# Scores of the 128-key units in three matmuls instead of five, low halves beside the mask, one rotary step a filler later

## Chip, cores and metric

The kernel runs on one core of a Trainium2 chip. The metric is the device time of the whole program in microseconds; before the change the median of 3 runs is 680.2 us (680.0 to 680.59).

## What is computed

The reference is one encoder block over 512 tokens of width 2048, in float32:

```
h = rms_norm(x);  a_q, a_k, a_v, a_g, b_cq, b_ckv, b_kr, b_g = split(h @ w_in)
A: sliding window attention, 16 heads of 64, window 128 in chunks of 64, one sink logit per head
B: qb = rms_norm(b_cq) @ w_q_b -> 8 heads x (128 "nope" + 64 rotary)
   kvb = rms_norm(b_ckv) @ w_kv_b -> 8 heads x (128 key + 128 value); one rotary key (64) for all heads
   s = (q_nope . k_nope + q_rope . k_rope) / sqrt(192)
   s = -1e30 where key chunk > query chunk (chunks of 64);  p = softmax(s);  o = p @ v
out = rms_norm(x + concat(A * silu(a_g), B * silu(b_g)) @ w_out)
```

## The kernel before

Float32 accuracy is kept with halves: each operand is split in a high part (rounded to the matmul's format fp32r) and a low part (the rest), and a product is three matmuls, high x high, low x high, high x low (`three`, L1076). ScalarE makes the high halves, VectorE or GpSimd the low ones. Weights come as a stream of 128x1024 chunks: a DMA into `w_raw`, ScalarE's `w_hi` (L364), GpSimd's `w_lo` (L283).

The order of work on each engine is written out by hand; every engine waits on semaphores only. The input projections and branch A come first (to about 402 us), then branch B, then the output projection (up to the end), each fed by the same stream.

Branch B has 8 heads in 4 pairs (pair 0 to 3), and a pair has 8 score units. Unit w = 8p + u has query block i = u % 4 of head u // 4, and 128 (i + 1) keys, because later keys are masked. So units with u = 0 and u = 4 have 128 keys, 8 units in the whole kernel. In the last 128 keys of a unit the upper right 64x64 quarter (queries of the first chunk, keys of the second) is masked. For one unit the steps are these:
- S (`b_score`): TensorE writes the scores to bank 4 + u % 2: two matmuls with the rotary parts (`qr` holds high and low query halves stacked on the 128 partitions, so two matmuls with `kr_hi` and `kr_lo` do the product), and three with the nope parts. It first waits for the probabilities of unit w - 2, which frees the bank.
- `b_maxima` (VectorE, L942): adds the mask `mask_b` (bf16, 0 or -1e30), negates, writes back to PSUM and reduces to the negated row maximum.
- `b_expo` (ScalarE, L526): exponential with that bias, row sums accumulated.
- `b_normalise` (VectorE): reciprocal (L948) and scaled probabilities `pb` (L951).
- T (`b_transpose`, L1329): TensorE transposes `pb`; `ptb_hi` by ScalarE (L534), `ptb_lo` by VectorE (L956).
- `b_product` (V0 after T3 for the first head; step L, in the next pair, for the second), taken by VectorE at L962.

`B_STEPS` is the order for all engines: S0 F S1 L F T0 S2 F T1 S3 F T2 S4 F T3 S5 F S6 F V0 T4 S7 F T5 F T6 F T7 F. F0 to F10 are fillers: on TensorE the projections of the next pair (in pair 3 the first tiles of the output projection), on ScalarE and GpSimd splits of those projections and of weight chunks, on VectorE the rotary work for the next pair in six parts (`b_rotary`; parts 0 to 3 are L907, part 4 is L909 and frees a bank, part 5 is the sum L912). `B_ROTARY` says which parts stand in which filler. VectorE does the normalisation of a unit after the filler (or before the next maximum). In a filler that follows S4, the rotary parts therefore stand ahead of the normalisation of unit 4. The rotary halves of the query are `b_rotary_high` (ScalarE, L505) and `b_rotary_low` (VectorE, L932). The transposes wait for these: T6 goes to bank 5 and so also for the probabilities of unit 7; T0 to T3 for those of their own unit and the low half of the transposed unit before.

`kr_hi` and `kr_lo` are two tensors of 512 columns, `kn_hi` and `kn_lo` four tensors (two per parity of the pair), each two heads by 512.

Of the kernel before, what the change touches and what calls it, by code (L numbers as in the profile page):

```python
# [6 lines left out]
ALU = mybir.AluOpType  # L7
ACT = mybir.ActivationFunctionType
AX = mybir.AxisListType
F32 = mybir.dt.float32  # L10
F32R = mybir.dt.float32r
# [3 lines left out]
P = 128  # L15
D_MODEL, SEQ = 2048, 512
CHUNK = 64
EPS = 1e-6
MASK_VALUE = -1e30
# [64 lines left out]
            {1: (14,), 4: (15,), 6: (16,), 8: (17,), 10: (18,)}]  # L84


B_ROTARY = [{3: (0,), 4: (1, 2), 5: (3,), 6: (4,), 7: (5,)}] + [{2: (0,), 3: (1,), 4: (2, 3), 5: (4,), 6: (5,)}] * 3
B_ROTARY_FIRST, B_ROTARY_SECOND, B_ROTARY_HIGH = 8, 1, (0, 1, 1, 0)
B_TAKE = (9, 7, 7, 7)

# [6 lines left out]
def build(nc, w_stream, x_t, x_nat, gains, final_w, tables, out):  # L97
    with ExitStack() as ctx:
        def sem(name):
            return ctx.enter_context(nc.semaphore(name))  # L100

        def bank(name):
            return ctx.enter_context(nc.psum_tensor(name, [P, 512], F32))
# [4 lines left out]
        def at(name, shape, dt, offset):  # L108
            return nc.alloc_sbuf_tensor_at(name, shape, dt, offset=offset)

        def region(nbytes):
            start = place[0]
            place[0] += (nbytes + 31) // 32 * 32
            return start
# [6 lines left out]
        KB = 1024  # L121
# [25 lines left out]
        mask_b = at("mask_b", [P, SEQ], BF16, r_consts)  # L147
# [4 lines left out]
        st_b = at("st_b", [P, 4, 4], F32, region(64))  # L152
# [12 lines left out]
        fw = at("fw", [P, D_MODEL], F32, r_ckv)  # L165
        r_cq = region(8192)
        cq = at("cq", [P, CQ_T, SEQ], F32, r_cq)
        kr_hi = at("kr_hi", [P, SEQ], F32R, region(2048))
        kr_lo = at("kr_lo", [P, SEQ], F32R, region(2048))
        r_tmp = region(6144)  # L170
        t1 = at("t1", [P, SEQ], F32, r_tmp)
        t2 = at("t2", [P, SEQ], F32, r_tmp + 2048)
# [19 lines left out]
        k_dup = at("k_dup", [P, A_KV_HEADS, SEQ], F32, r4 + 26 * KB + 512)  # L192
        v_f = at("v_f", [P, A_CHUNKS, P], F32, r4 + 30 * KB + 512)

        qn_hi, qn_lo, kn_hi, kn_lo, qr, vb_hi, vb_lo = ([] for _ in range(7))
        for par, r in enumerate((r_x, r4)):
            for n, (kept, name) in enumerate(((qn_hi, "qn_hi"), (qn_lo, "qn_lo"), (kn_hi, "kn_hi"), (kn_lo, "kn_lo"), (qr, "qr"))):
                kept.append(at(f"{name}{par}", [P, 2, SEQ], F32R, r + 4 * KB * n))
            vb_hi.append(at(f"vb_hi{par}", [P, TOK, 2 * P], F32R, r + 20 * KB))
            vb_lo.append(at(f"vb_lo{par}", [P, TOK, 2 * P], F32R, r + 24 * KB))  # L200
        pb = at("pb", [P, 4, SEQ], F32, r4 + 28 * KB)

        m_at = [r_cq, r_x, r_x + 8 * KB, r_x + 16 * KB, r_x + 32 * KB, r_x + 40 * KB, r_x + 24 * KB, r_x + 48 * KB]
# [3 lines left out]
        junk = at("junk", [P, SEQ], F32, r4 + 32 * KB)  # L207
        y_gained = at("y_gained", [P, SEQ], F32, r4 + 34 * KB)
        fin_t = at("fin_t", [P, 4], F32, region(16))
        HALF, BY_ACT = SEQ // 2, 896  # L210
        assert place[0] <= nc.sbuf_usable_end, place[0]

# [4 lines left out]
        B = [bank(f"bank{i}") for i in range(8)]  # L217
# [22 lines left out]
        gate_silu, gated = sem("gate_silu"), sem("gated")  # L240
        cqs_split, b_hi, b_lo = sem("cqs_split"), sem("b_hi"), sem("b_lo")
        b_rot_evac, b_rot, b_rot_hi, b_rot_lo = sem("b_rot_evac"), sem("b_rot"), sem("b_rot_hi"), sem("b_rot_lo")
        b_mask, b_scores, b_max, b_exp, b_recip, b_probs = sem("b_mask"), sem("b_scores"), sem("b_max"), sem("b_exp"), sem("b_recip"), sem("b_probs")
        b_turned, b_pt_hi, b_pt_lo, b_pv, b_out = sem("b_turned"), sem("b_pt_hi"), sem("b_pt_lo"), sem("b_pv"), sem("b_out")
        m_hi, m_lo, m_lo_pool = sem("m_hi"), sem("m_lo"), sem("m_lo_pool")
# [112 lines left out]
        def _(act):  # L358
# [111 lines left out]
            for t in range(4):  # L470
                for hf in range(17):
# [14 lines left out]
                    if hf in LATENT_AT and t == 3:  # L486
                        act.wait_ge(w_used, GT0 + 28)
                        k = LATENT_AT[hf]
# [7 lines left out]
                for ct in range(4):  # L496
                    act.wait_ge(gate_evac, 4 * t + (TOK + ct + 1))
                    dst = gate_tmp[:, ct, :] if ct < 2 else mixed[:, 2 * t + A_TILES + ct - 2, :]
# [23 lines left out]
            def b_expo(w):  # L522
                u = w % 8
                n = P * (u % 4 + 1)
                act.wait_ge(b_max, w + 1)
                act.activation(B[4 + u % 2][:, 0:n], B[4 + u % 2][:, 0:n], ACT.Exp, bias=st_b[:, u % 4, 0:1], scale=-1.0,  # L526
                               accum_out=st_b[:, u % 4, 2:3]).then_inc(b_exp, 1)
# [34 lines left out]
            for p in range(PAIRS):  # L562
                f = 0
                for step in B_STEPS:
                    w = 8 * p + (int(step[1]) if step[0] in "ST" else 0)
# [81 lines left out]
        def _(dve):  # L647
# [21 lines left out]
            for j in range(8):  # L669
                w_low(j)  # L670
                for h in range(2):
                    k = 2 * j + h
# [189 lines left out]
            for t in range(4):  # L862
# [24 lines left out]
                for ct in range(4):  # L887
# [3 lines left out]
                    dst = gate_tmp[:, ct, :] if ct < 2 else mixed[:, 2 * t + A_TILES + ct - 2, :]  # L891
# [5 lines left out]
            def b_rotary(p, part):  # L897

                bk, own = B[(PB_TILES * p + TILE_POS[4]) % 4], min(p, 1)
                if part == 0:  # L900
                    dve.wait_ge(proj_done, T_PB + PB_TILES * p + TILE_POS[4] + 1)
                    dve.wait_ge(rot_landed, 32 * own + 32)
                    if p > 0:
                        dve.wait_ge(b_rot_lo, 2 * p)
                if part < 4:
                    o = part ^ 1
                    dve.tensor_tensor(t2[32 * part:32 * part + 32, :], bk[32 * o:32 * o + 32, :], sin_b[own][32 * part:32 * part + 32, :], ALU.mult)  # L907
                elif part == 4:
                    dve.tensor_tensor(t1[:, :], bk[:, :], cos_b[own][:, :], ALU.mult).then_inc(b_rot_evac, 1)  # L909
                else:  # L910
                    dve.wait_ge(b_rot_evac, p + 1)
                    dve.tensor_tensor(t3[:, :], t1[:, :], t2[:, :], ALU.add).then_inc(b_rot, 1)  # L912
# [22 lines left out]
            def b_maxima(w):  # L935
                u = w % 8
                n = P * (u % 4 + 1)
                dve.wait_ge(b_scores, w + 1)


                sc = B[4 + u % 2][:, 0:n]
                dve.tensor_tensor_reduce(sc, sc, mask_b[:, SEQ - n:], -1.0, 3e38, ALU.add, ALU.min, st_b[:, u % 4, 0:1]).then_inc(b_max, 1)  # L942

            def b_normalise(w):
                u = w % 8
# [19 lines left out]
            dve.memset(mask_b[:, :], 0.0).then_inc(b_mask, 1)  # L965
            dve.wait_ge(b_mask, 1)
            dve.memset(mask_b[0:CHUNK, SEQ - CHUNK:], MASK_VALUE).then_inc(b_mask, 1)
            for part in range(6):
                b_rotary(0, part)
            dve.wait_ge(b_mask, 2)  # L970
# [7 lines left out]
            for p in range(PAIRS):  # L978
                f, late = 0, None
                for step in B_STEPS:  # L980
                    w = 8 * p + (int(step[1]) if step[0] in "ST" else 0)
                    if step[0] == "S":
                        if late is not None:
                            b_normalise(late)
                        b_maxima(w)
                        late = w
                        continue
# [11 lines left out]
                    else:  # L999
                        if p < PAIRS - 1:  # L1000
                            for part in B_ROTARY[p].get(f, ()):
                                b_rotary(p + 1, part)
# [72 lines left out]
        def _(pe):  # L1075
            def three(dst, ah, al, bh, bl, start, stop, frees_chunk=False):  # L1076

                ins = pe.matmul(dst, ah, bh, start=start, stop=False)  # L1078
                if frees_chunk:
                    ins.then_inc(w_used, int(frees_chunk))  # L1080
                pe.matmul(dst, al, bh, start=False, stop=False)  # L1081
                return pe.matmul(dst, ah, bl, start=False, stop=stop)  # L1082
# [218 lines left out]
            def b_score(w):  # L1301
                h, i, par = w % 8 // 4, w % 4, w // 8 % 2
                n = P * (i + 1)
                if w >= 2:
                    pe.wait_ge(b_probs, w - 1)
                if w % 8 == 1 and w > 1:
                    pe.wait_ge(b_pt_lo, w - 1)
                if i == 0:
                    pe.wait_ge(b_rot_lo, 2 * (w // 8) + h + 1)
                    pe.wait_ge(b_lo, 6 * (w // 8) + (2, 4)[h])  # L1310
                dst = B[4 + w % 2][:, 0:n]
                q = slice(P * i, P * i + P)
                pe.matmul(dst, qr[par][:, h, q], kr_hi[:, 0:n], start=True, stop=False)  # L1313
                pe.matmul(dst, qr[par][:, h, q], kr_lo[:, 0:n], start=False, stop=False)  # L1314
                three(dst, qn_hi[par][:, h, q], qn_lo[par][:, h, q], kn_hi[par][:, h, 0:n], kn_lo[par][:, h, 0:n], False, True).then_inc(b_scores, 1)
# [47 lines left out]
            for p in range(PAIRS):  # L1363
                f = 0
# [122 lines left out]
```

## Time and profile before

| | us |
|---|---|
| median of the runs | 680.2 |
| profiled execution | 680.3 |
| its span | 678.5 |
| VectorE busy | 338.9 |
| ScalarE busy | 305.4 |
| GpSimd busy | 303.1 |
| branch B's units, first score to last product | 402 to 519 |
| pairs begin (S0) | 402.5, 427.3, 454.4, 481.5 |

The mean granted clock is 0.997 of full speed. A busy TensorE here is a sum over instructions whose ends are modelled and which overlap; a stretch's cost is better read from the spacing of the starts. In rows of the timeline the first number is the start, the second the duration, and what stands in brackets at the end is idle time of the engine before it and what ended it.

### The profile page before, as it was taken

How to read it: one execution, taken by the hardware profiler on the slowest of the kernel's cores; microseconds unless marked ns; L12 is line 12 of the kernel's file. 1: busy time of each engine (PE TensorE's matmuls, PEld its weight loads, DVE VectorE, ACT ScalarE, POOL GpSimd, SP SyncE). 2: the span in 40 equal slices, each digit the busy share in tenths (PEclk: the TensorE clock that was granted, in tenths of full speed). 3: DMA queues.
4: the chain of work that ended last, by engine and by line, in shares of the span. 5: the costliest groups of instructions: out<-in, count | busy, mean ns of one | idle time of the engine just before them, and what ended most of it. 6: DMA issues, size and time to landing. Idle time of an engine off the chain costs nothing.

```text
span 678.5 us, 8917 instructions
## 1 busy us (share of the span) xinstructions
PE 669.2 (99%) x3196; PEld 559.8 (83%) x3196; DVE 338.9 (50%) x600; ACT 305.4 (45%) x574; POOL 303.1 (45%) x145
## 2 busy tenths in 40 slices
PE   9999999999999999999999999999999999999995
PEld 8888888888888888888888888888888888888884
DVE  5857132989784645645545578778651100101013
ACT  7723231321343664564465476666754321312233
POOL 0044443354253432532443445556866584464720
PEclk9999999999999999999999999999999999999998
DMA  8632322223222212222321412102124733223215
GB/s 320 233 118 93 111 96 94 91 95 102 84 94 94 93 63 94 93 68 90 101 85 63 155 61 97 63 31 95 32 89 173 290 115 108 93 93 99 88 60 219
DMA packets 21877, 73.54 MB, mean 108 GB/s; under 512 B 2384, under 2 KB 2640, under 8 KB 21712
## 3 DMA queue, kind: packets, MB, share of 16 engines
q1 hardware_dynamic: 18144, 65.61, 28.6%
q10 hardware_dynamic: 3696, 7.43, 3.0%
q8 instruction: 24, 0.39, 0.2%
q14 instruction: 13, 0.11, 0.1%
HBM read 68.83 MB, written 4.19 MB: 108 GB/s over the span
## 4 chain that ended last, share of the span: by engine, by line
PE 93%; DVE 3%; ACT 1%; issue 1%; DMA 1%; DVEq 0%; SPq 0%; ACTq 0%
PE bank L1082 29%; PE bank L1078 29%; PE bank L1081 28%; PE bank L1210 1%; PE bank L1220 1%; PE bank L1329 1%; DMA xs<-x_t 1%; PE bank L1313 1%; PE bank L1232 1%; PE bank L1233 1%; DVE ptb_lo L956 1%; DVE bank L942 1%; PE bank L1101 1%; PE bank L1098 1%; PE bank L1314 0%
## 5 line engine op out<-in xcount | busy, mean ns | idle before, releaser
L283 POOL TENSOR_TENSOR w_lo<-w_raw,w_hi 128x1024 fp32r<-128x1024 f32 x100 | 243.1, 2436 | 317.4 <-ACT w_hi L364 317.4
L364 ACT ACTIVATE w_hi<-w_raw 128x1024 fp32r<-128x1024 f32 x110 | 116.2, 1056 | 208.5 <-PE bank L1078 175.3
L1078 PE MATMUL bank<-x_hi,w_hi 128*128 128x512 f32 x504 | 196.9, 391 | 0.0
L1082 PE MATMUL bank<-x_lo,w_hi 128*128 128x512 f32 x504 | 196.7, 390 | 0.0
L1081 PE MATMUL bank<-x_hi,w_lo 128*128 128x512 f32 x504 | 196.2, 389 | 0.0
L1082 PEld LDWEIGHTS bank<-x_lo,w_hi 128*128 128x128 f32 x504 | 94.6, 188 | 20.1
L1078 PEld LDWEIGHTS bank<-x_hi,w_hi 128*128 128x128 f32 x504 | 94.7, 188 | 18.8 <-DVE mixed L892 0.5
L1081 PEld LDWEIGHTS bank<-x_hi,w_lo 128*128 128x128 f32 x504 | 94.7, 188 | 18.6
L1078 PE MATMUL bank<-w_hi,mx_hi 128*128 128x512 f32 x256 | 100.5, 393 | 0.0
L1081 PE MATMUL bank<-w_hi,mx_lo 128*128 128x512 f32 x256 | 100.0, 391 | 0.0
L1082 PE MATMUL bank<-w_lo,mx_hi 128*128 128x512 f32 x256 | 99.8, 390 | 0.0
L1031 DVE TENSOR_TENSOR y<-bank,y 128x512 f32 (+1 forms) x15 | 10.4, 692 | 123.7 <-PE bank L1082 123.7
L1082 PEld LDWEIGHTS bank<-w_lo,mx_hi 128*128 128x128 f32 x256 | 48.1, 188 | 10.4
L1078 PEld LDWEIGHTS bank<-w_hi,mx_hi 128*128 128x128 f32 x256 | 48.1, 188 | 10.2 <-POOL w_lo L283 0.3
L1081 PEld LDWEIGHTS bank<-w_hi,mx_lo 128*128 128x128 f32 x256 | 48.1, 188 | 9.8
L454 ACT ACTIVATE bank<-pa,st_a 128x128 f32<-128x128 f32 x64 | 22.8, 356 | 43.1 <-DVE st_a L806 43.1
L526 ACT ACTIVATE bank<-bank,st_b 128x128 f32<-128x128 f32 (+3 forms) x32 | 16.1, 502 | 29.3 <-DVE st_b L942 29.0
L709 DVE TENSOR_TENSOR t<-bank,sin_r 32x512 f32<-32x512 f32 x40 | 27.5, 687 | 0.5
L821 DVE TENSOR_TENSOR pta_lo<-bank,pta_hi 128x512 fp32r<-128x512 f32 x16 | 11.1, 692 | 31.9 <-ACT pta_hi L461 31.8
L829 DVE TENSOR_TENSOR mixed<-bank,o_low 64x256 f32<-64x256 f32 x32 | 13.5, 423 | 22.1 <-ACT o_low L468 21.8
L956 DVE TENSOR_TENSOR ptb_lo<-bank,ptb_hi 128x128 fp32r<-128x128 f32 (+3 forms) x32 | 15.6, 487 | 14.0 <-ACT ptb_hi L534 14.0
L461 ACT ACTIVATE pta_hi<-bank 128x512 fp32r<-128x512 f32 x16 | 9.6, 598 | 22.8 <-PE bank L1220 22.8
(209 smaller groups left out, 928.9 us busy)
## 6 DMA issues: line engine op xcount, KB each, us to landing
w_raw<-w_stream SPq DMA_DIRECT2D x110, 512.0 KB, 3.3
y<-x_nat ACTq DMA_DIRECT2D x4, 1024.0 KB, 10.5
out<-y SPq DMA_DIRECT2D x6, 512.0 KB, 3.1
xs<-x_t SPq DMA_DIRECT2D x4, 512.0 KB, 5.2
mixed<-x_t SPq DMA_DIRECT2D x4, 512.0 KB, 5.1
fw<-final_w ACTq DMA_DIRECT2D x1, 1024.0 KB, 18.7
cos_b<-tables ACTq DMA_DIRECT2D x2, 256.0 KB, 2.8
sin_b<-tables ACTq DMA_DIRECT2D x2, 256.0 KB, 3.1
```

What stands on the lines that cost most here:

```text
L283: pool.tensor_tensor(w_lo[:, s % HL, :], w_raw[:, s % RAW, :], w_hi[:, s % HL, :].bitcast(F32), ALU.subtract)\
L364: act.activation(w_hi[:, s % HL, :], w_raw[:, s % RAW, :], ACT.Copy).then_inc(w_hi_ready, 1)
L454: act.activation(B[4][:, P * k:P * k + P], pa[:, slot, k, :], ACT.Exp, bias=st[:, 1, k:k + 1], scale=A_SCALE, accum_out=st[:, 3, k:k + 1])
L526: act.activation(B[4 + u % 2][:, 0:n], B[4 + u % 2][:, 0:n], ACT.Exp, bias=st_b[:, u % 4, 0:1], scale=-1.0, accum_out=st_b[:, u % 4, 2:3]) ...
L709: ins = dve.tensor_tensor(t2[32 * q:32 * q + 32, :], src[32 * o:32 * o + 32, :], sin[32 * q:32 * q + 32, :], ALU.mult)
L821: dve.tensor_tensor(pta_lo[:, :], B[6][:, :], pta_hi[:, :].bitcast(F32), ALU.subtract).then_inc(a_pt_lo, 1)
L829: ins = dve.tensor_tensor(out_e, by_head[h, e], o_low[h, :, :, :], ALU.add)
L956: dve.tensor_tensor(ptb_lo[:, 0:i + 1, P * i:P * i + P], turned(w).rearrange("p (a b) -> p a b", a=i + 1), ptb_hi[:, 0:i + 1, P * i:P * i ...
L1031: dve.tensor_tensor(ys, B[t][:, :], ys, ALU.add).then_inc(o_evac, 1)
L1078: ins = pe.matmul(dst, ah, bh, start=start, stop=False)
L1081: pe.matmul(dst, al, bh, start=False, stop=False)
L1082: return pe.matmul(dst, ah, bl, start=False, stop=stop)
```

## The change

It does four things.
1. `kr_hi` and `kr_lo` become the two halves of one tensor `kr_parts`, and `kn_hi` and `kn_lo` of one `kn_parts` per parity. Addresses of the other tensors of a pair stay.
2. In a unit of 128 keys the matmul with `qr` moves 256 columns, high and low keys side by side, into columns 0 to 127 and 128 to 255 of the bank, and so does the matmul with `qn_hi`. The one with `qn_lo` takes high keys only. The scores are the sum of the two halves.
3. ScalarE copies the low half (columns 128 to 255) to a new SBUF tensor `low_scores`, 128x128, in two activations that leave the masked quarter alone; that quarter holds -1e30 from one memset at the start of branch B. VectorE's maximum takes `low_scores` in place of the mask, after waiting for the copies. On ScalarE the copies stand at the unit's S step, ahead of its exponential, and wait for the scores.
4. `B_ROTARY`: the filler with two parts becomes the next one. In pair 0 from {4: (1, 2), 5: (3,)} to {4: (1,), 5: (2, 3)}, in pairs 1 and 2 from {4: (2, 3), 5: (4,)} to {4: (2,), 5: (3, 4)}. The entry of pair 3 is not used, as there is no next pair.

```diff
-B_ROTARY = [{3: (0,), 4: (1, 2), 5: (3,), 6: (4,), 7: (5,)}] + [{2: (0,), 3: (1,), 4: (2, 3), 5: (4,), 6: (5,)}] * 3
+B_ROTARY = [{3: (0,), 4: (1,), 5: (2, 3), 6: (4,), 7: (5,)}] + [{2: (0,), 3: (1,), 4: (2,), 5: (3, 4), 6: (5,)}] * 3
...
-        kr_hi = at("kr_hi", [P, SEQ], F32R, region(2048))
-        kr_lo = at("kr_lo", [P, SEQ], F32R, region(2048))
+        kr_parts = at("kr_parts", [P, 2, SEQ], F32R, region(4096))
+        kr_hi, kr_lo = kr_parts[:, 0, :], kr_parts[:, 1, :]
...
+            kn_parts.append(at(f"kn_parts{par}", [P, 2, 2, SEQ], F32R, r + 8 * KB))
...
+        low_scores = at("low_scores", [P, P], F32, region(512))
...
             def b_expo(w):
                 u = w % 8
                 n = P * (u % 4 + 1)
+                if u % 4 == 0:
+                    if w == 0:
+                        act.wait_ge(b_mask, 3)
+                    act.wait_ge(b_scores, w + 1)
+                    low = B[4 + u % 2][:, P:2 * P]
+                    act.activation(low_scores[:, 0:CHUNK], low[:, 0:CHUNK], ACT.Copy).then_inc(b_low_kept, 1)
+                    act.activation(low_scores[CHUNK:, CHUNK:], low[CHUNK:, CHUNK:], ACT.Copy).then_inc(b_low_kept, 1)
...
-                sc = B[4 + u % 2][:, 0:n]
-                dve.tensor_tensor_reduce(sc, sc, mask_b[:, SEQ - n:], -1.0, 3e38, ALU.add, ALU.min, st_b[:, u % 4, 0:1]).then_inc(b_max, 1)
+                sc, added = B[4 + u % 2][:, 0:n], mask_b[:, SEQ - n:]
+                if u % 4 == 0:
+                    dve.wait_ge(b_low_kept, w // 2 + 2)
+                    added = low_scores[:, :]
+                dve.tensor_tensor_reduce(sc, sc, added, -1.0, 3e38, ALU.add, ALU.min, st_b[:, u % 4, 0:1]).then_inc(b_max, 1)
...
+            dve.memset(low_scores[0:CHUNK, CHUNK:], MASK_VALUE).then_inc(b_mask, 1)
...
+                if i == 0:
+                    by_part = B[4 + w % 2][:, 0:2 * P].rearrange("p (l k) -> p l k", l=2)
+                    pe.matmul(by_part, qr[par][:, h, q], kr_parts[:, :, 0:P], start=True, stop=False)
+                    pe.matmul(by_part, qn_hi[par][:, h, q], kn_parts[par][:, :, h, 0:P], start=False, stop=False)
+                    pe.matmul(dst, qn_lo[par][:, h, q], kn_hi[par][:, h, 0:P], start=False, stop=True).then_inc(b_scores, 1)
+                    return
```

## Rows read from the trace of the kernel before

**Rows 1.** The page: busy time, share of the span, instructions, by engine.
```profile
PE 669.2 (99%) x3196; PEld 559.8 (83%) x3196; DVE 338.9 (50%) x600; ACT 305.4 (45%) x574; POOL 303.1 (45%) x145
```

**Rows 2.** Waits, 395 to 520 us: in total, times, longest.
```profile
PEld bank L1313 <- DVE pb L951: 2.0, 3, 0.8
```

**Rows 3.** Timeline, TensorE, S4 of pair 1 (128 keys).
```profile
439.00 0.28 PE L1078 MATMUL bank<-kn_hi,qn_hi 128*128 128x128 f32 x1
439.11 0.27 PE L1081 MATMUL bank<-kn_hi,qn_lo 128*128 128x128 f32 x1
439.22 0.28 PE L1082 MATMUL bank<-kn_lo,qn_hi 128*128 128x128 f32 x1
```

**Rows 4.** Chain of waits in time order: start, length, what (branch A's scores).
```profile
205.76 0.48 PE bank L1210 x4
```

**Rows 5.** Timeline, ScalarE, small copies from PSUM.
```profile
222.26 0.38 ACT L468 ACTIVATE o_low<-bank 64x256 f32<-64x256 f32 x1
...
433.85 0.26 ACT L534 ACTIVATE ptb_hi<-bank 128x128 fp32r<-128x128 f32 x1
```

**Rows 6.** Timeline, S0 of pair 0: last matmul, maximum.
```profile
402.87 0.27 PE L1082 MATMUL bank<-kn_lo,qn_hi 128*128 128x128 f32 x1
...
403.30 0.30 DVE L942 CUSTOM_DVE_ANT_0 bank<-bank,mask_b 128x128 f32<-128x128 f32 x1 [2.00 <-PE bank L1082]
```

**Rows 7.** Timeline, pair 0: pb of unit 3, weight load of T3.
```profile
412.86 0.75 DVE L951 TENSOR_SCALAR pb<-bank,st_b 128x512 f32<-128x512 f32 x1
...
413.67 0.14 PEld L1329 LDWEIGHTS bank<-ident,pb 128*128 128x128 f32 x1
```

**Rows 8.** Timeline, pair 0: ptb_lo of unit 3, pb of unit 7, T6.
```profile
417.28 0.69 DVE L956 TENSOR_TENSOR ptb_lo<-bank,ptb_hi 128x512 fp32r<-128x512 f32 x1 [0.95 <-ACT ptb_hi L534]
...
424.24 0.75 DVE L951 TENSOR_SCALAR pb<-bank,st_b 128x512 f32<-128x512 f32 x1
...
425.14 0.52 PE L1329 MATMUL bank<-ident,pb 128*128 128x128 f32 x3
```

**Rows 9.** Rotary sum: its line (min/median/max ns); pair 1 timeline beside GpSimd.
```profile
L912 DVE TENSOR_TENSOR t<-t,t x4: 694/1585/1793, 395.8 to 473.5; 128x512 f32<-128x512 f32 x4
...
446.37 1.29 POOL L297 TENSOR_TENSOR kn_lo<-b_tmp,kn_hi 128x512 fp32r<-128x512 f32 x1 [1.90 <-ACT kn_hi L520]
...
446.42 1.79 DVE L912 TENSOR_TENSOR t<-t,t 128x512 f32<-128x512 f32 x1
```

**Rows 10.** Timeline, S0 of pair 1: ScalarE's split, maximum.
```profile
428.06 1.05 ACT L364 ACTIVATE w_hi<-w_raw 128x1024 fp32r<-128x1024 f32 x1
...
428.81 0.29 DVE L942 CUSTOM_DVE_ANT_0 bank<-bank,mask_b 128x128 f32<-128x128 f32 x1
```

**Rows 11.** Timeline, pair 1: rotary low half, GpSimd's next operation, T1.
```profile
432.89 1.75 DVE L932 SCALAR_TENSOR_TENSOR qr<-t,qr 64x512 fp32r<-64x512 f32 x1 [0.22 <-ACT qr L505]
...
434.05 2.86 POOL L283 TENSOR_TENSOR w_lo<-w_raw,w_hi 128x1024 fp32r<-128x1024 f32 x1
...
435.71 0.41 PE L1329 MATMUL bank<-ident,pb 128*128 128x128 f32 x2
```

**Rows 12.** Timeline, pair 1, S4 to S6, three engines.
```profile
440.31 0.48 ACT L534 ACTIVATE ptb_hi<-bank 128x384 fp32r<-128x384 f32 x1
...
441.29 0.29 DVE L942 CUSTOM_DVE_ANT_0 bank<-bank,mask_b 128x128 f32<-128x128 f32 x1
...
441.67 1.40 DVE L907 TENSOR_TENSOR t<-bank,sin_b 32x512 f32<-32x512 f32 x2
...
443.28 0.35 DVE L951 TENSOR_SCALAR pb<-bank,st_b 128x128 f32<-128x128 f32 x1
...
443.69 0.44 PE L1313 MATMUL bank<-kr_hi,qr 128*128 128x384 f32 x1 [0.32 <-DVE pb L951]
```

**Rows 13.** Timeline, pair 1: pb of unit 7, T6.
```profile
451.20 0.75 DVE L951 TENSOR_SCALAR pb<-bank,st_b 128x512 f32<-128x512 f32 x1
...
452.26 0.49 PE L1329 MATMUL bank<-ident,pb 128*128 128x128 f32 x3
```

More of the change, by code:

```diff
@@ L193, in build @@
         v_f = at("v_f", [P, A_CHUNKS, P], F32, r4 + 30 * KB + 512)
-        qn_hi, qn_lo, kn_hi, kn_lo, qr, vb_hi, vb_lo = ([] for _ in range(7))
+        qn_hi, qn_lo, kn_parts, qr, vb_hi, vb_lo = ([] for _ in range(6))
         for par, r in enumerate((r_x, r4)):
-            for n, (kept, name) in enumerate(((qn_hi, "qn_hi"), (qn_lo, "qn_lo"), (kn_hi, "kn_hi"), (kn_lo, "kn_lo"), (qr, "qr"))):
+            for n, (kept, name) in ((0, (qn_hi, "qn_hi")), (1, (qn_lo, "qn_lo")), (4, (qr, "qr"))):
                 kept.append(at(f"{name}{par}", [P, 2, SEQ], F32R, r + 4 * KB * n))
+            kn_parts.append(at(f"kn_parts{par}", [P, 2, 2, SEQ], F32R, r + 8 * KB))
             vb_hi.append(at(f"vb_hi{par}", [P, TOK, 2 * P], F32R, r + 20 * KB))
             vb_lo.append(at(f"vb_lo{par}", [P, TOK, 2 * P], F32R, r + 24 * KB))
+        kn_hi, kn_lo = ([parts[:, n, :, :] for parts in kn_parts] for n in range(2))
         pb = at("pb", [P, 4, SEQ], F32, r4 + 28 * KB)
@@ L242, in build @@
         b_rot_evac, b_rot, b_rot_hi, b_rot_lo = sem("b_rot_evac"), sem("b_rot"), sem("b_rot_hi"), sem("b_rot_lo")
+        b_low_kept = sem("b_low_kept")
         b_mask, b_scores, b_max, b_exp, b_recip, b_probs = sem("b_mask"), sem("b_scores"), sem("b_max"), sem("b_exp"), sem("b_recip"), sem("b_probs")
```

## The prediction

> **What bounds the kernel now.** The page first: TensorE is busy for 669.2 of 678.5 us [rows 1], so only shorter work on TensorE, or a shorter wait of TensorE, moves the end. The change lies in branch B, 402 to 519 us. There I read TensorE's waits (the weight load waits, since it stands ahead of its matmul): score units waited 2.0 us in three places for the scaled probabilities of an earlier unit [rows 2], part of it under matmuls that still ran. What a wait costs I take from the starts: before S6 of pair 1 the last filler matmul (512 columns, 0.23 to the next start) began at 442.97, so S6 was due at 443.20 and came at 443.69 [rows 12]: 0.49. S6 of pair 2 is the same 27.1 us later; S6 of pair 0 shows 0.17, and four transposes 0.12 to 0.16 each. So TensorE is the bound with little to spare, and VectorE and ScalarE run a chain of small steps right behind it. Both must be followed.
>
> **TensorE.** A unit of 128 keys is five matmuls of 128 columns, starts 0.11 apart [rows 3]: 0.55. It becomes two of 256 and one of 128. Matmuls of 256 columns whose moving operand is two separate runs of 128, as it will be here, are in the trace already: branch A's scores, four in 0.48 [rows 4], 0.12 each. 0.12 + 0.12 + 0.11 = 0.35, so 0.20 less, in 8 units: 1.60 us. Bounds: 0 (if only columns counted, 640 before and after) and 0.22.
> The Trainium skill, "TensorE: Matmul & The Clock Gate", section Back-to-back issue gap, speaks against the change: an isolated warm gap of 134 cycles for 128 columns and 262 for 256 makes it 5 x 134 = 670 against 2 x 262 + 134 = 658 cycles, nothing. The rows go against it: 128 columns start 110 ns apart, not 56, and 256 cost hardly more. The same page gives a load of 128 weight columns as 107 ns, which fits the 110.
>
> **The new step on ScalarE.** Two activations, 128x64 and 64x64, PSUM to SBUF. A 128x128 copy takes 0.26, a 64x256 one 0.38 [rows 5], so I take some 0.23 each. In sequence that is 0.46, overlapped 0.36. Bounds for both: 0.2 and 0.76 (twice the 64x256). VectorE's maximum now waits for them. Its second operand, four-byte low scores for the two-byte mask, I cost at nothing (one pass over 128 columns; between 0 and 0.1). The one memset more has cover: VectorE idles 2.00 just before the first maximum [rows 6].
>
> **Pair 0, S0.** The last matmul runs 402.87 to 403.14 and the maximum starts at 403.30 [rows 6], a hop of 0.16. Now it ends at 402.94, the first copy starts at 403.10 (ScalarE has nothing to do then), the copies end between 403.46 and 403.56, the maximum starts some 0.05 later: 0.30 late (bounds 0.1 and 0.6). Behind it VectorE and ScalarE hand on to each other almost without idle (maximum, exponential, vb split, next maximum, ...), so pb of unit 3, which ended at 413.61, ends at 413.91. The weight load of T3 started at 413.67, 0.06 behind it [rows 7], so T3 was just in time, 0.19 behind the end of pb. TensorE, 0.4 sooner after S0 and S4, would like T3 at 413.4 and gets it at 414.10. Both savings of pair 0 are lost, and 0.30 more. Copies at S4 cost nothing here, as in pair 1 below. The wait of 0.17 at S6 goes (one rotary step less ahead of its pb), leaving +0.13.
> Then the moved step. From 417.28 to 424.99 (pb of unit 7) VectorE is almost solid [rows 8]. It now starts 0.30 later and holds one more 0.69 at filler 5. It gets back 0.2 of idle and part of the stall of the rotary sum (L912 takes 0.69 alone, up to 1.79 beside GpSimd [rows 9]). So pb of unit 7 comes 0.1 to 0.8 later; T6 was released by it (424.99, T6 at 425.14) and moves with it. I take +0.40 for pair 0, near the middle, since both the idle and the stall must come back in full for the lower end. If the copies take 0.76, it is +0.7.
>
> **Pairs 1 and 2.** They repeat each other 27.1 us apart; I work pair 1. At S0 ScalarE does a w_hi split first (428.06 to 429.11), and the maximum stood at 428.81 [rows 10]. It now waits for copies that start at about 429.0: at 429.41, 0.60 later, and so are the vb splits and the rotary high half. But the rotary low half (432.89) sat 1.75 instead of 0.69, until GpSimd went from one operation to the next at 434.05 [rows 11]. Started at 433.5 it gets in at the same 434.05. It can't miss that gap: GpSimd's next operation needs a w_hi split that ScalarE does after the rotary high half. So VectorE is back on its old times from there. T1 waits for the low half of the transposed unit 0, which follows that chain, and stays at 435.71 [rows 11]; the 0.20 of S0 is lost in front of it.
> The Trainium skill, "SBUF — State Buffer", on the port pair that VectorE and GpSimd share, says that a VectorE operation with two SBUF inputs waits for the whole of a running GpSimd operation; by that too the low half ends at 434.64 at whichever moment before 434.05 it is issued. The rows agree.
> At S4 ScalarE is free at 440.79, the maximum began at 441.29 because VectorE was late [rows 12]: the copies end at about 441.2, no cost. TensorE keeps the 0.20 of S4. Two rotary steps (1.40) stood ahead of pb of unit 4 (443.28 to 443.63), for which S6 waited [rows 12]. With one, pb ends at about 442.93, and TensorE wants S6 at 443.0: the wait of 0.49 goes. S6 is 0.69 sooner. The displaced step puts pb of unit 5 0.7 later, to 446.65; S7 wants it at 447.26. Behind it the rotary sum (446.42) stood until GpSimd ended at 447.66 [rows 9]; begun at 447.05 it ends at the same 448.21. S7's maximum waited for TensorE, so pb of unit 7 (451.95 [rows 13]) moves only 0.35 sooner, to 451.60, T6 follows at 451.79 instead of 452.26: pair 1 gives -0.47, pair 2 the same. Bounds for each: -0.90 (no wait anywhere, all savings) and +0.6 (the moved 0.69 reaches T6).
>
> **Pair 3** has no rotary work, no moved step and no wait of TensorE in its timeline: 2 x 0.20 = -0.40. Behind it TensorE is never idle until the last stage, so what branch B gives stays given.
>
> **Sum.** +0.40 - 0.47 - 0.47 - 0.40 = -0.94. The profiled execution took 680.3 us (span 678.5 and 1.8 around it), so 679.36; the runs' median is 680.2, 0.1 under it: 679.3.
>
> **Rivals.**
> A, everything arrives: 1.60, and 0.17 + 0.49 + 0.49 and some 0.3 of small waits: 2.75, 677.5. For it: ScalarE idles before the first copies, and if they overlap T3 is late by less. Against: T3 had nothing to spare and wants to be 0.4 sooner, so pb of unit 3 would have to come sooner too, and nothing shortens its chain. A half way (T3 and T1 hold TensorE less, 678.5) belongs here. Chance 0.22.
> B, slower: the moved 0.69 lands on TensorE. Place: fillers 5 to 7, pb of unit 7, for which T6 waits (0.12 to spare in pair 1). Price: +0.6 in each of pairs 0, 1, 2, less 0.40 in pair 3: +1.4, 681.6; with one pair spared, 681.0. It decides once the rotary sum starts after GpSimd's gap at 447.66 (now 446.42, forecast 447.05), so with 0.6 more of delay. For it: GpSimd runs long operations there. Against: those rows. Chance 0.11.
> C, the change doesn't shorten TensorE's work: the price goes by columns, 640 before and after. Then pair 3 gives 0, pairs 1 and 2 only the S6 waits less what T6 takes back, -0.3 each, pair 0 +0.4: 680.0. Against: [rows 4] (four such matmuls in 0.48). Chance 0.05. (It is what the isolated gaps of the Trainium skill's page "TensorE: Matmul & The Clock Gate" give.)
> D, no change: T1, T3 and T6 give back nearly all in pairs 0 to 2, -0.1 each, and the copies at 0.76 make pair 0 +0.7: with pair 3, 680.3. Chance 0.15.
> Forecast: 0.47.
>
> **Numbers.** What can be told from no change is 0.2%, 1.36 us: under 678.84 is faster, over 681.56 slower. Faster: A and the lower edge of the forecast, 0.31. Slower: half of B, 0.05. Within: 0.64. Range 678.0 to 680.8: it leaves out the full A and most of B.
>
> **What would show it.** Right: in unit S0 of every pair two score matmuls of 256 and one of 128, starts 0.12 apart; first maximum 0.2 to 0.4 later; T3 of pair 0 released by VectorE's pb, about 0.3 later; no wait at S6 of pairs 1 and 2, but at T6; rotary low half and rotary sum of pairs 1 and 2 ending where GpSimd's operations end. Wrong: copies of over 0.4 each, a wait at S7, matmuls of 256 spaced over 0.15, GpSimd or weight chunks later, or a T3 of pair 0 that starts sooner than before.

## The result and the profile after

| | before | after |
|---|---|---|
| median of 19 runs each, us | 680.33 | 681.61 |
| profiled execution | 680.3 | 681.65 |
| its span | 678.5 | 679.9 |

The ratio is 1.0018, 95% interval 1.0012 to 1.0025: slower by 1.28 us, about 0.2%. Forecast was 679.3, with a range to 680.8. Both the sign and the range were wrong.

Part 1 of the page of the changed kernel (busy time, share, instructions), against [rows 1], with four rows of its waits, 395 to 520 us (total, times, longest), against [rows 2]:

```profile
PE 668.4 (98%) x3180; PEld 558.7 (82%) x3180; DVE 336.2 (49%) x601; ACT 308.3 (45%) x590; POOL 303.0 (45%) x145
...
PEld bank L1352 <- DVE pb L967: 5.1, 8, 1.1
DVE bank L958 <- ACT low_scores L537: 4.5, 4, 2.4
PE bank L1352 <- DVE pb L967: 1.7, 3, 0.7
PE bank L1352 <- DVE ptb_lo L972: 1.1, 2, 0.6
```

In the kernel before, the same view had for the transposes:

```profile
PEld bank L1329 <- DVE pb L951: 0.9, 3, 0.4
```

TensorE has 16 instructions and 0.8 us of busy time less and a span 1.4 longer: it waits more. The waits have moved from the score units (L1313 before) to the transposes (L1329 before, L1352 now).

The clearest view is one that I worked out from the timelines: the start of each TensorE step minus its start in the kernel before, called its shift from here on. A difference that appears between two lines is what the steps between them cost (when it grows) or gave (when it falls). Each profiled execution enters branch B with an offset of its own from what lies ahead of it (line S1 shows it; where S0 is one pass, 0.20 must be added to it). The experiments below are the other columns: e1, rotary table only; e4, both copies only; e9, one copy only; e3, one pass without copies, new table; e12, the same with the old table; e11, the changed kernel with the split first; e13, the best one. Line "end" is the first matmul of the last product.

```
us    step after  e1    e4    e9    e3    e12   e11   e13
404.4 S1   -0.04 -0.14  0.04  0.12 -0.17 -0.06 -0.14 -0.03
413.8 T3    0.56 -0.13  0.66  0.32 -0.31 -0.20  0.48 -0.03
416.4 S6    0.46 -0.31  0.79  0.45 -0.43 -0.07  0.37 -0.03
423.3 T5    0.69 -0.28  0.77  0.44 -0.31 -0.09  0.61 -0.06
425.1 T6    1.43  0.51  0.82  0.44  0.48 -0.09  1.36 -0.05
427.3 S0'1  1.44  0.51  0.82  0.45  0.48 -0.09  1.36 -0.05
433.2 T0'1  1.23  0.52  0.81  0.45  0.27 -0.30  1.15 -0.26
435.7 T1'1  1.82  0.52  1.21  0.49  0.48 -0.09  1.03 -0.38
440.8 T3'1  1.62  0.53  1.21  0.49  0.28 -0.29  0.80 -0.61
443.7 S6'1  1.14  0.04  1.20  0.48 -0.22 -0.09  0.32 -1.10
452.3 T6'1  1.38  0.00  1.24  0.51 -0.04 -0.05  0.52 -0.90
454.4 S0'2  1.42  0.04  1.25  0.51  0.00 -0.04  0.57 -0.86
462.8 T1'2  1.80  0.04  1.62  0.54 -0.03 -0.05  0.25 -1.18
470.8 S6'2  1.10 -0.46  1.62  0.53 -0.72 -0.05 -0.48 -1.90
479.4 T6'2  1.63 -0.21  1.64  0.53 -0.28 -0.07 -0.03 -1.46
481.5 S0'3  1.91  0.08  1.64  0.53  0.01 -0.07  0.25 -1.18
484.9 S1'3  1.70  0.07  1.65  0.54 -0.21 -0.27  0.03 -1.39
516.2 end   1.50  0.09  1.65  0.53 -0.41 -0.48 -0.17 -1.59
```

(S6'1 is S6 of pair 1; without a mark it is pair 0.) In the changed kernel each unit of 128 keys saves 0.20 to 0.22 (S0'1 to T0'1, S0'3 to S1'3), S6'1 and S6'2 lose their wait of about 0.5, and pair 3 gives 0.41. All of that is overtaken at T3 (with S4's saving lost in front of it), T6, T1'1 with T1'2, and T6'2 to S0'3. One more place is not in the table: S7 of pair 0 starts at 421.34, where 420.68 was its start before (0.66), and waits there for pb of unit 5. It costs 0.20 against S6. With the old table the kernel with both copies loses nothing there, so this is the moved step too.

**T3.** Timeline of the changed kernel, S0 of pair 0 and T3, against [rows 6, 7]:

```profile
402.75 0.28 PE L1333 MATMUL bank<-kn_parts,qn_hi 128*128 128x256 f32 x1
402.87 0.22 PE L1334 MATMUL bank<-kn_parts,qn_lo 128*128 128x128 f32 x1
403.19 0.22 ACT L536 ACTIVATE low_scores<-bank 128x64 f32<-128x64 f32 x1
403.51 0.22 ACT L537 ACTIVATE low_scores<-bank 64x64 f32<-64x64 f32 x1
403.91 0.30 DVE L958 CUSTOM_DVE_ANT_0 bank<-bank,low_scores 128x128 f32<-128x128 f32 x1 [2.39 <-ACT low_scores L537]
...
413.56 0.75 DVE L967 TENSOR_SCALAR pb<-bank,st_b 128x512 f32<-128x512 f32 x1
414.36 0.66 PE L1352 MATMUL bank<-ident,pb 128*128 128x128 f32 x4 [0.63 <-DVE pb L967]
```

Each copy takes 0.22, as forecast. But they don't overlap: they start 0.32 apart here (0.24 at the other units), and the maximum starts 0.18 behind the second one's end. From the end of the last score matmul to the maximum it is 0.82, not 0.16. The maximum is 0.61 later than before, 0.46 without the offset of 0.15, against 0.30 forecast. pb of unit 3 is 0.70 later (0.55 without it), and T3 waits for it. The 0.09 between 0.46 and 0.55 is a second price of the copies; it arises in the exponential right behind them and is shown below at T1.

**T6.** The same kernel's timeline around T6, against [rows 8]:

```profile
423.74 1.28 POOL L303 TENSOR_TENSOR qn_lo<-b_tmp,qn_hi 128x512 fp32r<-128x512 f32 x1 [1.65 <-ACT qn_hi L526]
...
424.09 1.48 DVE L925 TENSOR_TENSOR t<-t,t 128x512 f32<-128x512 f32 x1
...
425.68 0.75 DVE L967 TENSOR_SCALAR pb<-bank,st_b 128x512 f32<-128x512 f32 x1
...
426.57 0.52 PE L1352 MATMUL bank<-ident,pb 128*128 128x128 f32 x3 [0.74 <-DVE pb L967]
```

And the kernel before:

```profile
422.29 1.29 POOL L297 TENSOR_TENSOR qn_lo<-b_tmp,qn_hi 128x512 fp32r<-128x512 f32 x1 [0.98 <-ACT qn_hi L520]
...
422.74 1.39 DVE L912 TENSOR_TENSOR t<-t,t 128x512 f32<-128x512 f32 x1
```

There GpSimd's operation ran 422.29 to 423.58 and the rotary sum 422.74 to 424.13. Now they start 1.45 and 1.35 later, and the sum stalls as long as before. I had counted on the stall to absorb the moved step. It moves along instead, because GpSimd's operation waits for a ScalarE split, and this split stands behind the late exponential of unit 6.

**T1 of pair 1**, timeline of the changed kernel, against [rows 10, 11]:

```profile
429.50 1.05 ACT L370 ACTIVATE w_hi<-w_raw 128x1024 fp32r<-128x1024 f32 x1
430.45 0.21 ACT L536 ACTIVATE low_scores<-bank 128x64 f32<-128x64 f32 x1
430.69 0.22 ACT L537 ACTIVATE low_scores<-bank 64x64 f32<-64x64 f32 x1
431.05 0.30 DVE L958 CUSTOM_DVE_ANT_0 bank<-bank,low_scores 128x128 f32<-128x128 f32 x1 [0.72 <-ACT low_scores L537]
...
431.44 0.34 ACT L539 ACTIVATE bank<-bank,st_b 128x128 f32<-128x128 f32 x1 [0.54 <-DVE st_b L958]
...
431.91 0.58 ACT L521 ACTIVATE b_tmp<-bank 128x512 f32<-128x512 f32 x1
...
434.63 1.29 POOL L303 TENSOR_TENSOR vb_lo<-b_tmp,vb_hi 128x512 fp32r<-128x512 f32 x1 [0.28 <-ACT vb_hi L526]
435.24 1.23 DVE L945 SCALAR_TENSOR_TENSOR qr<-t,qr 64x512 fp32r<-64x512 f32 x1 [1.34 <-ACT qr L511]
...
437.53 0.41 PE L1352 MATMUL bank<-ident,pb 128*128 128x128 f32 x2 [0.55 <-DVE ptb_lo L972]
```

The kernel before, the exponential of unit 0 and the next activation:

```profile
429.19 0.34 ACT L526 ACTIVATE bank<-bank,st_b 128x128 f32<-128x128 f32 x1
...
429.55 0.59 ACT L515 ACTIVATE b_tmp<-bank 128x512 f32<-128x512 f32 x1
```

The maximum stands 2.24 later than before and the pair began 1.44 later: 0.80 of delay, not 0.60. Then comes the second price: from the start of the exponential to that of the next activation it is 0.47, where it was 0.36. All 128-key units with both copies have 0.46 to 0.47, in every kernel; all without copies, and those with the 128x64 copy alone, 0.35 to 0.36. So the second copy, on 64 partitions, makes the ScalarE step behind it 0.1 longer. The second vb split of ScalarE is 0.90 late and keeps GpSimd waiting (0.28 of idle), so GpSimd's operation, and with it the rotary low half of VectorE, ends 0.39 later than the pair's shift accounts for, and T1 starts 0.38 later.

### The profile page after: what moved, and what is told of

Read it like the earlier page. It is cut to its first block, busy times and chain, and to the rows that moved or that the text cites. A ratio compares the mean times of both kernels' runs of the same rounds, so it can differ in the third digit from the quotient of the medians.

```text
span 679.9 us, 8910 instructions
## 1 busy us (share of the span) xinstructions
PE 668.4 (98%) x3180; PEld 558.7 (82%) x3180; DVE 336.2 (49%) x601; ACT 308.3 (45%) x590; POOL 303.0 (45%) x145
## 4 chain that ended last, share of the span: by engine, by line
PE 88%; DVE 5%; ACT 4%; issue 2%; DMA 0%; ACTq 0%; DVEq 0%
PE bank L1099 27%; PE bank L1095 27%; PE bank L1098 27%; PE bank L1227 1%; PE bank L1237 1%; DVE bank L958 1%; PE bank L1352 1%; ACT w_hi L370 1%; DVE pb L967 1%; PE bank L1132 1%; ACT bank L539 1%; DVE t L920 1%; DVE ptb_lo L972 1%; PE bank L1249 1%; PE bank L1250 1%
```

## Experiments

Times are medians of 10 to 12 runs, each against runs of the kernel before on the same chip (680.25 to 680.43 in the four batches); the ratio's 95% interval reaches 0.0009 or 0.0010 to both sides, some 0.6 us. So only five experiments are told from before by their times: one pass with the old table, copies only, three units, pair 2 too, and the best one. For the others the reading rests on the shifts, each from one profiled execution; they agree with the medians within 0.3 once each one's offset is out.

**Rotary table only.** Kernel before, with

```diff
-B_ROTARY = [{3: (0,), 4: (1, 2), 5: (3,), 6: (4,), 7: (5,)}] + [{2: (0,), 3: (1,), 4: (2, 3), 5: (4,), 6: (5,)}] * 3
+B_ROTARY = [{3: (0,), 4: (1,), 5: (2, 3), 6: (4,), 7: (5,)}] + [{2: (0,), 3: (1,), 4: (2,), 5: (3, 4), 6: (5,)}] * 3
```

> The kernel before with the new rotary table alone. Theory 1 (the loss of pair 0 has two parts: the two copies of S0 delay the chain to T3, and the moved rotary step delays pb of unit 7 and T6): here the copies are missing, so T3 of pair 0 stays at its old place, S6 of pairs 1 and 2 loses its wait of 0.49 each, T6 takes part of that back, pair 0 loses up to 0.3: 0.4 to 0.9 us faster than before. Rival (the moved step alone is what costs, since VectorE has no room for it in fillers 5 to 7): T6 of pair 0 about 0.7 later and little gained in pairs 1 and 2: the same or up to 0.8 slower.

Measured 680.42 against 680.32, ratio 1.0002. Theory 1 had 0.4 to 0.9 faster and failed: T3 stays (right) and pair 1 gains 0.47, but T6 of pair 0 is 0.79 later against T5, where I had said 0.3 at most, and pair 2 gives back 0.54 between S6'2 and S0'3. The rival was right for pair 0, wrong for pair 1. From the timeline of this kernel at T6, the same picture without any copy:

```profile
422.80 1.29 POOL L297 TENSOR_TENSOR qn_lo<-b_tmp,qn_hi 128x512 fp32r<-128x512 f32 x1 [1.64 <-ACT qn_hi L520]
...
423.15 1.49 DVE L912 TENSOR_TENSOR t<-t,t 128x512 f32<-128x512 f32 x1
...
424.75 0.75 DVE L951 TENSOR_SCALAR pb<-bank,st_b 128x512 f32<-128x512 f32 x1
...
425.65 0.52 PE L1329 MATMUL bank<-ident,pb 128*128 128x128 f32 x3 [0.79 <-DVE pb L951]
```

**One pass with copies, old table.** The changed kernel with the `-` line above.

> The changed kernel with the old rotary table. Theory 1: T3 of pair 0 0.55 later than before as in the changed kernel, S6 waits in pairs 0, 1 and 2 are back and move by the delay of the chain; per pair about +0.7, +0.3, +0.5 and -0.4 in pair 3: 1.0 to 1.6 slower than before, about level with the changed kernel. Rival (the moved step alone costs): 1 us or more faster than the changed kernel.

Measured 681.18 against 680.32, ratio 1.0012: 0.86 slower, a little less than said; 0.43 under the changed kernel (0.27 by the shifts). So within the changed kernel the new table costs a little on balance: by the shifts it costs 0.70 in pair 0 and gives 0.43 in pair 1. Here S6 of pair 1 is not 0.5 sooner but 0.2 later against T3.

**No copies.** The changed kernel with

```diff
-                    act.wait_ge(b_scores, w + 1)
-                    low = B[4 + u % 2][:, P:2 * P]
-                    act.activation(low_scores[:, 0:CHUNK], low[:, 0:CHUNK], ACT.Copy).then_inc(b_low_kept, 1)
-                    act.activation(low_scores[CHUNK:, CHUNK:], low[CHUNK:, CHUNK:], ACT.Copy).then_inc(b_low_kept, 1)
...
-                    dve.wait_ge(b_low_kept, w // 2 + 2)
-                    added = low_scores[:, :]
```

> The changed kernel without ScalarE's copies and without the low half of the keys in the sum (it is computed by TensorE and dropped; the maximum adds the mask as before), so the scores of the 128-key units are less exact. Theory 1: TensorE's saving with no delay of the first maximum. T3 of pair 0 about 0.2 sooner than before, S6 of pairs 1 and 2 0.7 sooner, pair 3 0.4 sooner: 1.0 to 1.8 faster than before, so 2.2 to 3 us below the changed kernel. Rival (moved step alone costs): 0 to 0.5 faster than before. Rival (256 columns in two runs save TensorE nothing): pair 3 unchanged.

The low halves of the keys are computed and not added, so the scores of the 128-key units are less exact. Measured 679.93 against 680.32, ratio 0.9994 (0.9985 to 1.0003). So within the changed kernel the copies cost 1.67 us (1.28 + 0.39; 1.79 by the shifts). But the gain is 0.4, not 1.0 to 1.8: my theory's figure failed here too, at T6 of pair 0 (0.79 lost between T5 and T6) and in pair 2.

**Copies only.** Five matmuls, old table, the copies of the diff above added as they are in the changed kernel, and VectorE waiting for them.

> The kernel before (five matmuls, old rotary table) with the two copies of ScalarE added in each 128-key unit and VectorE waiting for them; they copy columns nobody needs and the maximum adds the mask. Theory 1: the bare price of the copies: T3 of pair 0 0.7 to 0.9 later, T1 of pairs 1 and 2 0.4 to 0.6 later, pair 3 unchanged: 1.5 to 2.2 slower than before. Rival (moved step alone costs): within 0.4 of before.

Measured 681.75 against 680.32, ratio 1.0022 (1.0013 to 1.0031): 1.43 slower, just under the theory's 1.5 to 2.2. It arises at T3 (0.62), S6 (0.13), T1'1 (0.40) and T1'2 (0.37), hardly anywhere else; pair 3 doesn't mind the copies. What is copied here is of no use to the scores: only the time counts.

**One copy only.** The kernel above without the second activation.

> The kernel before with one of the two copies (128x64) added in each 128-key unit, VectorE waiting for it, five matmuls, old rotary table, the mask added as before. Theory 1 (the price is the delay of the first maximum of a pair, handed on): about 0.24 less delay at each S0 than with both copies, so 0.2 less at T3 of pair 0 and at T1 of pairs 1 and 2: 0.6 to 1.0 slower than before, against 1.4 with both. Rival (the wait across the engines is the price, the copies' length is not): 1.3 to 1.5 slower, as with both.

Measured 680.69 against 680.26, ratio 1.0005. 0.43 instead of 1.43, less than the theory said, because T1'1 and T1'2 are not late at all (0.04, 0.03). Pairs 1 and 2 have room for about one copy and none for two: here GpSimd goes from the first vb low half to the second without a gap, where it waited 0.28 in the kernel with both copies only, as in the changed kernel. The second copy costs more than its start 0.24 later: without it the next activation after the exponential comes 0.35 behind it, not 0.46.

**Sum later.** New table in the kernel before, and in pair 0 the rotary sum in filler 8:

```diff
-{3: (0,), 4: (1,), 5: (2, 3), 6: (4,), 7: (5,)}
+{3: (0,), 4: (1,), 5: (2, 3), 6: (4,), 8: (5,)}
```

> The kernel before with the new rotary table, and in pair 0 the rotary sum (part 5) one filler later still, in filler 8, behind the normalisation of unit 7. Theory 1 (refined by the traces so far: the moved step makes unit 6's exponential late, ScalarE's and GpSimd's next split with it, and the sum, which stands ahead of pb of unit 7, waits for that GpSimd operation to end): T6 of pair 0 comes 0.3 to 0.8 sooner than in the kernel with the new table alone, with the rest of the kernel following: 679.6 to 680.2. Rival (VectorE simply has one step of 0.7 too much between T4 and T6, wherever the sum stands): T6 of pair 0 no more than 0.1 sooner, 680.4.

Measured 680.42 against 680.26, ratio 1.0001: level with the table alone. The time is the rival's (680.4), not the theory's (679.6 to 680.2). But at T6 it did what the theory said: by the shifts 0.36 is lost between T5 and T6, not 0.79. From its timeline:

```profile
423.51 1.28 POOL L297 TENSOR_TENSOR qn_lo<-b_tmp,qn_hi 128x512 fp32r<-128x512 f32 x1 [1.64 <-ACT qn_hi L520]
...
425.05 0.75 DVE L951 TENSOR_SCALAR pb<-bank,st_b 128x512 f32<-128x512 f32 x1
...
425.95 0.52 PE L1329 MATMUL bank<-ident,pb 128*128 128x128 f32 x3 [0.35 <-DVE pb L951]
426.05 0.68 DVE L912 TENSOR_TENSOR t<-t,t 128x512 f32<-128x512 f32 x1
```

The sum takes 0.68 once GpSimd is done, and pb doesn't stand behind it. But the rotary halves now come late: 0.11 was lost again at S0'1 and 0.18 at T1'1. So 0.43 of the 0.79 goes when the sum is out of the way, 0.36 stays with the moved step, and most of the 0.43 is lost again later.

**Old table in pair 0 alone**, otherwise the changed kernel.

> The changed kernel with the old rotary row in pair 0 alone (the new ones in pairs 1 and 2). Theory 1 (prices are pair by pair, and add): pair 0 as in the kernel with the old table, +0.6 instead of +1.3, pairs 1 to 3 as in the changed kernel: 0.4 to 0.8 faster than the changed kernel, 680.8 to 681.2. Rival (what one pair gives, the next takes back): within 0.2 of the changed kernel.

Measured 680.74 against 680.26, ratio 1.0006. 0.80 less over before than the changed kernel (0.59 by the shifts), at the edge of what was expected. T6 of pair 0 is no longer late against T5 (0.05, after 0.74), and pairs 1 to 3 cost and give what they did: prices add pair by pair.

**Three units.** `ONE_PASS = (12, 24, 28)` in place of `u % 4 == 0` (and of `i == 0`), and

```diff
+B_ROTARY = [{3: (0,), 4: (1, 2), 5: (3,), 6: (4,), 7: (5,)}, {2: (0,), 3: (1,), 4: (2,), 5: (3, 4), 6: (5,)}, {2: (0,), 3: (1,), 4: (2, 3), 5: (4,), 6: (5,)}, {}]
```

> One pass with the copies in units 12, 24 and 28 only (S4 of pair 1, both of pair 3), five matmuls elsewhere, and the new rotary row in pair 1 only. Theory 1: pair 0 and pair 2 as before, pair 1 -0.4 to -0.6 (the wait at S6 goes, the 0.2 of S4 is given back at T6), pair 3 -0.4 (no wait there): 0.7 to 1.1 faster than before. Rival (a copy delays something wherever it stands): no more than 0.4 faster.

Measured 679.36 against 680.26, ratio 0.9985 (0.9976 to 0.9994): 0.90 faster, as expected, 0.42 from pair 1 and 0.35 from pair 3 by the shifts. At S4 of pair 1 the copies cost nothing because VectorE comes late to that maximum anyway (441.31, before 441.29). In pair 3 they do delay the first maximum (483.41 against 483.00, with TensorE 0.39 ahead), but no step of TensorE was in need of it.

**Pair 2 too**, with the first split of `mixed` later:

```diff
-ONE_PASS = (12, 24, 28)
+ONE_PASS = (12, 20, 24, 28)
...
-                    if p == PAIRS - 2 and f in (6, 9):
+                    if p == PAIRS - 2 and f in (8, 9):
```

> As the kernel with one pass in units 12, 24 and 28 and the new rotary row in pair 1, and also in pair 2: unit 20 in one pass, the new rotary row, and the first split of mixed (mx_hi, mx_lo) moved from filler 6 to filler 8 on ScalarE and GpSimd. Theory 1 (pair 2 gave back its gain because that split, 1.06 us on ScalarE, stood between the late exponential of unit 22 and what T6 needs): pair 2 now gains as pair 1, 0.3 to 0.5 more: 1.2 to 1.5 faster than before, 678.8 to 679.1. Rival (the split is in the way in filler 8 too, on GpSimd beside the rotary low half): level with the kernel it starts from, 679.3, or slower.

Measured 680.96 against 680.43, ratio 1.0011: slower. The rival had the sign right, but the loss came by a third way. Pair 2 did gain (S0'3 at -0.74, against -0.39 in the kernel it starts from), and then TensorE lost 1.75 between S0'3 and S1'3. From its timeline:

```profile
480.59 4.72 POOL L310 TENSOR_TENSOR mx_lo<-mixed,mx_hi 128x1024 fp32r<-128x1024 f32 x2
...
483.05 0.47 PE L1096 MATMUL bank<-w_hi,mx_hi 128*128 128x512 f32 x1 [1.78 <-issue]
```

The first tile of the output projection needs the first `mx_lo`, which now ended at about 483.0. GpSimd works there without a gap in the kernel before (476.7 to 492.1), so a split moved back is time lost. The reason for the edit was real: with the split out of filler 6, T6 of pair 2 gave back 0.12 against T5, not 0.53 as in the changed kernel, and S0 of pair 3 nothing, not 0.24. The rotary low half shows why, in the changed kernel and then in this one:

```profile
480.36 2.38 POOL L309 TENSOR_TENSOR mx_lo<-mixed,mx_hi 128x1024 fp32r<-128x1024 f32 x1
...
481.21 2.08 DVE L945 SCALAR_TENSOR_TENSOR qr<-t,qr 64x512 fp32r<-64x512 f32 x1
```

```profile
478.80 0.68 DVE L946 SCALAR_TENSOR_TENSOR qr<-t,qr 64x512 fp32r<-64x512 f32 x1
```

S0 of pair 3 needs that half, and started at 483.39 in the changed kernel, 0.10 behind its end. But the cure was worse than the stall.

**Split first**: the changed kernel with the w_hi and w_lo split of filler 10 in filler 9.

```diff
-B_CHUNKS = [{2: (5,), 4: (6,), 10: (7,)}, {1: (8,), 3: (9,), 10: (10,)}, {1: (11,), 3: (12,), 10: (13,)},
+B_CHUNKS = [{2: (5,), 4: (6,), 9: (7,)}, {1: (8,), 3: (9,), 9: (10,)}, {1: (11,), 3: (12,), 9: (13,)},
```

> The changed kernel with the w_hi split (and GpSimd's w_lo) of filler 10 moved to filler 9, so that ScalarE's copies at S0 of pairs 1, 2 and 3 no longer stand behind a split of 1.06 us. Theory 1: the first maximum of pairs 1 and 2 comes 0.5 to 0.8 sooner against the rest, the second vb split is in time for GpSimd, and T1 of pairs 1 and 2 is 0.2 to 0.6 sooner each: 0.4 to 1.0 faster than the changed kernel. Rival (T1 is held by GpSimd's operations alone, not by the copies' place): within 0.2 of the changed kernel.

Measured 679.98 against 680.43, ratio 0.9993: 1.73 less over before than the changed kernel, more than expected. Between T0 and T1 of pair 1 it gains 0.12 where the changed kernel lost 0.59, of pair 2 0.11 (the changed kernel lost 0.60). From its timeline at S0 of pair 1:

```profile
429.43 0.22 ACT L536 ACTIVATE low_scores<-bank 128x64 f32<-128x64 f32 x1
429.67 0.22 ACT L537 ACTIVATE low_scores<-bank 64x64 f32<-64x64 f32 x1
430.17 0.29 DVE L958 CUSTOM_DVE_ANT_0 bank<-bank,low_scores 128x128 f32<-128x128 f32 x1
```

ScalarE used to idle 1.39 before `ptb_hi` of unit 7; the split now fills that, and the maximum no longer waits for the copies. This edit does a second thing: GpSimd's `w_lo` of the same chunk now runs at 428.57, not 430.63, and is out of the way when the first vb low half is due (432.16, after 1.18 of idle; in the changed kernel it came at 433.05, right behind `w_lo`). No run takes the two apart, so how much of the 1.73 is the copies' place stays open.

**One pass without copies, old table.**

> One pass in all eight units, without the copies and without the low half of the keys in the sum, old rotary table. It asks what TensorE's saving of 8 x 0.2 is worth by itself. Theory 1 (it arrives only where nothing waits): pair 3 -0.4, pair 0 -0.1 to -0.3 (the first maximum is 0.2 sooner), pairs 1 and 2 nothing, since T1 and S6 wait for VectorE: 0.4 to 0.7 faster than before. Rival (most of it arrives): 1.2 or more faster.

The scores are less exact here as well. Measured 680.07 against 680.43, ratio 0.9995 (0.9986 to 1.0004): 0.36 faster by the medians, which is inside the noise, and 0.62 by the shifts. So 1.6 us of TensorE time is worth 0.4 to 0.6 by itself: pair 3 gives 0.41; in pairs 1 and 2 each 0.20 is handed back at T1 and at S6; in pair 0 S0's 0.20 is kept and S4's is handed back, by S6.

**The best one**: pair 0 as before; in pairs 1 to 3 one pass with copies in every 128-key unit, the new rotary rows, the split in filler 9.

> Pair 0 as before (five matmuls, old rotary row, no copies); pairs 1, 2 and 3 with one pass and copies in all units of 128 keys, the new rotary rows, and the w_hi split of filler 10 in filler 9. Theory 1 (prices pair by pair, read at the start of each pair from the kernel with the split first): pair 0 0, pair 1 -0.8, pair 2 -0.3, pair 3 -0.4: 1.3 to 1.7 faster than before, 678.6 to 679.0. Rival (pair 1 gained in that kernel because pair 0 had left TensorE late and the others ahead): 0.9 faster or less, no better than one pass in three units.

Measured 678.73 against 680.25, ratio 0.9977 (0.9968 to 0.9987): 1.52 faster, in the middle of what was expected, and 2.80 better, each against before, than the changed kernel.

## Why the prediction was wrong

By its own steps; the offset of 0.15 with which the profiled execution entered branch B is taken out.

- TensorE, 0.20 for a unit: right (0.20 to 0.22). Rival C, a price by columns, is out. For a stream with a weight load each, the Trainium skill, "TensorE: Matmul & The Clock Gate", section Back-to-back issue gap, gives about 81 ns per matmul of 128 columns and about 131 ns for 512. The trace doesn't bear that out here: 110 ns for 128 [rows 3], and 230 ns for 512.
- The copies' length, 0.22 each: right. What was missed: they don't overlap (0.24 to 0.32 apart), there are 0.14 to 0.18 more to VectorE, not 0.05, and the exponential's step behind them is 0.1 longer, a term that the prediction doesn't have. The first maximum was 0.46 late (said 0.30), pb of unit 3 0.55, T3 0.41 late (0.30), S6 0.31 (0.13). A mis-sized term.
- "It gets back ... part of the stall of the rotary sum": the step that failed worst. Pair 0 cost 1.29 by T6 and not 0.40. The stall has no fixed time: it moved with the rest of the chain, 1.39 long before and 1.48 after. In the kernel with the table alone, T6 lost 0.79 against T5 to a moved step of 0.69: nothing was absorbed.
- "At the same 434.05", T1 of pair 1 as before: failed. The rotary low half did end where GpSimd's operations end, but those were 0.39 later, since the maximum was 0.80 late and the second vb split 0.90, and not 0.6. The prediction named the late vb splits but didn't follow them to GpSimd. Pairs 1 and 2 lost 0.38 each there.
- S6 of pairs 1 and 2, wait of 0.49 gone, and S4's copies free: right. T6 of pair 1 gave back 0.26 (0.22 said). Pair 1 came to -0.02 (said -0.47): what is left of the difference is T1 and that.
- "Pair 2 the same": failed. ScalarE does a split of 1.06 there in filler 6 that pair 1 doesn't have, and GpSimd a longer operation beside the rotary low half: T6 took back 0.53 and S0'3 0.24. Pair 2 came to +0.49. With that split moved (pair 2 too) they took back 0.12 and nothing.
- Pair 3, -0.40: right (-0.41).

1.29 - 0.02 + 0.49 - 0.41 = 1.35, against -0.94. Rival B's 681.6 is the measured time by luck: it had +0.6 in each of pairs 0 to 2. B (the moved step reaches T6 in pairs 0 to 2) was half the truth: it decided in pair 0 and, for another reason, in pair 2, and beside it stood the copies, with 1.67 us by the kernel without them. In pair 1 the moved step did what was forecast. B's chance of 0.11 was too low: I had seen that VectorE had hardly any idle time from 417 to 425 and that T6 waited for its last step.

One sum of the prediction is wrong in itself: rival A's terms, 1.60 + 0.17 + 0.49 + 0.49 + 0.3, make 3.05 and 677.2; 2.75 leaves the 0.3 of small waits out.

Open: why the first pair of copies starts 0.32 apart and the others 0.24, in every kernel that has both in unit 0; and why the second copy makes the exponential's step longer.

## What to carry over

A shorter stretch on the bound engine pays only where nothing behind it is just in time; here 1.6 us of it brought 0.4 to 0.6, and a hop over a third engine ahead of a chain that is just in time cost 1.4 to 1.8. A stall beside another engine can't be counted as room for added work until it is clear that what holds the other engine doesn't wait for the same chain. Look unit by unit: put the added step only where its consumer comes late anyway or where nothing bound waits for it, and move other work (the split) into idle time ahead of it. The same edits, left out of pair 0 and with the split moved, gave 1.52 us instead of costing 1.28.

## Unexpected of the hardware

Two activations of ScalarE from one PSUM bank to one tensor, on 128 and on 64 partitions, start 0.24 us apart though each takes 0.22, where others of ScalarE here overlap by about 0.1 (429.55 for 0.59 and the next at 430.03, before the change). An exponential with a row sum behind these two takes 0.46 to the next activation instead of 0.36, though ScalarE idles in between; behind the 128x64 one alone it takes 0.36. Whether the 64 partitions or the count of two does it, no run tells.

VectorE's maximum starts 0.14 to 0.18 after a copy's end, as it does after a score matmul's (0.16), whereas behind the row sum that ends ScalarE's exponential VectorE starts within 0.04.

An operation of VectorE with both inputs in SBUF (0.68 alone) took 1.48 beside a GpSimd operation that began 0.35 before it, and ended 0.55 after that one's end. The Trainium skill, "SBUF — State Buffer", section Who interferes with whom, says that a VectorE instruction with two SBUF inputs contends with a GpSimd instruction that reads SBUF, and that the one issued first blocks the other. The trace agrees, and in the kernel with the sum later the same sum, with no GpSimd operation beside it, took 0.68.
